# A two-block transformer kernel whose stage ends are reordered by token half, with five weight buffers instead of three

## The reference

```
x = layer_norm(ALPHA*x + rwkv7_time_mix(x)) ; x = layer_norm(ALPHA*x + swiglu_ffn(x))      # block 0
x = layer_norm(ALPHA*x + moba_attention(x)) ; x = layer_norm(ALPHA*x + swiglu_ffn(x))      # block 1
n = rmsnorm(x); z = n @ w_in -> conv branch, top-k attention branch, gates
h = x + (g_conv*y_conv + g_attn*y_attn) @ w_mix_out
h = h + cross_attention(rmsnorm(h), rmsnorm(mem)) @ wx_o
h = h + square(relu(rmsnorm(h) @ w_ff1)) @ w_ff2
return rmsnorm(h)
```

## Time and profile before

| | |
|---|---|
| median of 3 runs | 1526.9 us (1525.79 to 1529.86) |
| the profiled execution, its own time | 1531.04 us |
| its span, first to last instruction | 1528.9 us |
| mean granted TensorE clock | 0.965 |
| busy: PE, DVE, ACT, POOL | 1414.8, 882.3, 635.4, 78.6 us |
| weights and other data moved | 204.96 MB |

### The profile page before, as it was taken

The page is one execution under the profiler, slowest core; times in us unless marked ns, Lnnn a source line. Parts: engine busy times, 40 slices in busy tenths (PEclk is TensorE's granted clock), DMA queues, the critical chain, the costliest instruction groups (busy, mean ns, idle before and its releaser), DMA issues.

```text
span 1528.9 us, 21626 instructions
## 1 busy us (share of the span) xinstructions
PE 1414.8 (93%) x9280; PEld 1266.8 (83%) x9280; DVE 882.3 (58%) x1277; ACT 635.4 (42%) x899; POOL 78.6 (5%) x44
## 2 busy tenths in 40 slices
PE   7998999997899998999899999799988888799997
PEld 4676998996799997876689999798978887599996
DVE  4268426335644446555464444698998755465554
ACT  1342342433434433444453343534344545554443
POOL 0011120001200002100020000100000000000000
PEclk9999999998899999999999999898999999999999
DMA  9422000003555553623065555554543434255651
GB/s 287 139 73 83 1 29 1 1 29 110 166 193 193 180 192 107 211 83 111 28 227 192 188 193 166 161 157 131 166 145 111 156 120 129 91 184 175 195 192 69
DMA packets 154383, 204.96 MB, mean 134 GB/s; under 512 B 7440, under 2 KB 128400, under 8 KB 154160
## 3 DMA queue, kind: packets, MB, share of 16 engines
q1 hardware_dynamic: 154288, 203.59, 40.7%
HBM read 202.53 MB, written 1.05 MB: 133 GB/s over the span
## 4 chain that ended last, share of the span: by engine, by line
PE 69%; DVE 21%; ACT 6%; DMA 2%; issue 2%; DVEq 0%; SPq 0%; ACTq 0%
PE PS L468 16%; PE PS L469 16%; PE PS L470 16%; DVE PH L1963 6%; DVE WL L1541 4%; PE PS L756 3%; PE PS L743 3%; PE PS L760 2%; PE PS L659 2%; ACT WH L1082 2%; DMA RG<-in_ffn_w_in 1%; PE PS L604 1%; PE PS L709 1%; DVE PA L1775 1%; DMA RG<-in_moba_w_qkv 1%
## 5 line engine op out<-in xcount | busy, mean ns | idle before, releaser
L1541 DVE TENSOR_TENSOR WL<-RG,WH 128x2048 fp32r<-128x2048 f32 x163 | 372.5, 2290 | 246.1 <-ACT WH L1082 246.1
L468 PE MATMUL PS<-AH,WH 128*128 128x256 f32 x1664 | 482.7, 290 | 13.6 <-DVE AL L1568 9.5
L469 PE MATMUL PS<-AL,WH 128*128 128x256 f32 x1664 | 477.8, 287 | 0.0
L470 PE MATMUL PS<-AH,WL 128*128 128x256 f32 x1664 | 477.2, 287 | 0.0
L1082 ACT ACTIVATE WH<-RG 128x2048 fp32r<-128x2048 f32 x164 | 311.9, 1907 | 134.1 <-PE PS L470 87.9
L468 PEld LDWEIGHTS PS<-AH,WH 128*128 128x128 f32 x1664 | 326.1, 196 | 21.0 <-issue 11.8
L469 PEld LDWEIGHTS PS<-AL,WH 128*128 128x128 f32 x1664 | 326.3, 196 | 1.6 <-issue 0.2
L470 PEld LDWEIGHTS PS<-AH,WL 128*128 128x128 f32 x1664 | 326.0, 196 | 0.0
L468 PE MATMUL PS<-WH,HH 128*128 128x512 f32 x304 | 118.8, 391 | 0.0
L469 PE MATMUL PS<-WL,HH 128*128 128x512 f32 x304 | 118.8, 391 | 0.0
L470 PE MATMUL PS<-WH,HL 128*128 128x512 f32 x304 | 118.4, 389 | 0.0
(11 more groups left out here) (272 smaller groups left out, 1796.1 us busy)
## 6 DMA issues: line engine op xcount, KB each, us to landing
RG<-in_ffn_w_in SPq DMA_DIRECT2D x44, 1024.0 KB, 5.1
RG<-in_w_ff SPq DMA_DIRECT2D x32, 1024.0 KB, 5.4
RG<-in_w_in SPq DMA_DIRECT2D x30, 1024.0 KB, 5.2
RG<-in_ffn_w_down SPq DMA_DIRECT2D x22, 1024.0 KB, 4.9
RG<-in_moba_w_qkv SPq DMA_DIRECT2D x12, 1024.0 KB, 5.9
RG<-in_w_rkv SPq DMA_DIRECT2D x7, 1024.0 KB, 5.5
PA<-in_w_rkv SPq DMA_DIRECT2D x5, 1024.0 KB, 5.2
RG<-in_w_o SPq DMA_DIRECT2D x4, 1024.0 KB, 6.2
```

The lines of the kernel that those rows point to most:

```text
L468: e.matmul(o, lh, rh, start=start, stop=False)
L469: e.matmul(o, lh, rl, start=False, stop=False)
L470: return e.matmul(o, ll, rh, start=False, stop=stop)
L1541: v.tensor_tensor(WL[:, lo_n % NW, :], ring(SPLIT[lo_n]), WH[:, lo_n % NW, :].bitcast(F32), ALU.subtract).then_inc(s_lo, 1)
```

## The change

Six things change together.

1. Every stage end finishes the first half of the tokens before the second. `wo2`/`wo3`, `mo2`/`mo3`, `mx2`/`mx3`, `xo0`/`xo1`, and the last two down pieces of each FFN run as (piece a, half 0), (piece b, half 0), (piece a, half 1), (piece b, half 1).
2. DVE norms half 0 at once, then takes the remainder of the next stage's first weight, then norms half 1. The RMS norms work on one half at a time; DVE scales both halves (before, ACT scaled the second).
3. The memory unit that stood before the transposes of `ln0`, `ln1`, `ln2` now stands between the two halves. Its PSUM bank is another, and a wait on its copy-out inside the transposes is gone.
4. All pieces use five ring buffers, in a tensor of their own.
5. The final norm is per half, with one DVE instruction for scale and gain; POOL takes no part.
6. The DMA scratch of the program is set to 256 (it pays for the two buffers).

```diff
-    _k = _i % 5 if _n in EARLY else _i % 3
+    _k = _i % 5
...
-        RG = ctx.enter_context(nc.sbuf_tensor("RG", [128, 3, 2048], F32))
+        RG = ctx.enter_context(nc.sbuf_tensor("RG", [128, 5, 2048], F32))
...
-        MEM_AT = [PS[3][:, 0:256], PS[4][:, 0:256]] * 3 + [PS[3][:, 0:256], PS[2][:, 0:256]]
+        MEM_AT = [PS[5][:, 0:256], PS[4][:, 0:256]] * 4
...
+            def token_last(names, banks, nk=8):
+
                 for tt in range(2):
+                    for kp, name in enumerate(names):
+                        if tt == 0:
+                            split_ready(name)
+                        token_piece(name, banks[tt], tt, kp, nk)
+
+            def to_chan(name, src, banks, between=None):
+                for tt in range(2):
+                    if tt and between is not None:
+                        mem_unit(between)
...
-                        if tt == 0 and k == (4 if name == 'nmix' else 6) and name in MEM_BEFORE:
-                            e.wait_ge(s_mkvo, MEM_BEFORE[name])
...
+                    if 1 <= j < n - 1:
+                        down(f, n, j - 1, 0, mem_units)
+                        down(f, n, j - 1, 1, mem_units)
+                for tt in range(2):
+                    down(f, n, n - 2, tt, mem_units)
+                    down(f, n, n - 1, tt, mem_units)
...
-            token(('wo2', 'wo3'), (5, 7))
-            mem_unit(0)
-            to_chan('ln0', S1, [0, 1, 2, 3])
+            token_last(('wo2', 'wo3'), (5, 7))
+            to_chan('ln0', S1, [0, 1, 2, 3], 0)
...
-            def rms_scaled(q):
-                s.wait_ge(s_rv, q + 1)
-                s.activation(ST[:, 60:62], ST[:, 60:62], ACT.Sqrt, bias=0.0, scale=1.0).then_inc(s_rsd, 1)
-                s.wait_ge(s_rr_, q + 1)
-                s.activation(S1[:, 1, :], H[:, 1, :], ACT.Copy, bias=0.0, scale=ST[:, 61:62]).then_inc(s_na, 1)
+            def rms_std(q, tt):
+                s.wait_ge(s_rv, 2 * q + tt)
+                s.activation(ST[:, 60 + tt:61 + tt], ST[:, 60 + tt:61 + tt], ACT.Sqrt, bias=0.0, scale=1.0).then_inc(s_rsd, 1)
...
                 v.wait_ge(s_ho, half_mm)
                 ln_part(0, 0)
-                piece_done(first)
-                ln_part(1, 0)
                 v.wait_ge(s_ho, half_mm + 1)
                 ln_part(0, 1)
                 ln_scale(q, 0)
+                ahead(f'ln{q}', 1)
+                piece_done(first)
+                ln_part(1, 0)
                 piece_done(second)
                 ln_part(1, 1)
                 ln_scale(q, 1)
...
+            def final(tt):
...
+                for h in range(2):
+                    sl = slice(h * 512, h * 512 + 512)
+                    v.scalar_tensor_tensor(out=S1[:, tt, sl], in0=H[:, tt, sl], scalar=ST[:, c], in1=ring('nfin')[:, sl],
+                                           op0=ALU.mult, op1=ALU.mult).then_inc(s_fin, 1)
...
-    nc = _bacc.Bacc("TRN2", target_bir_lowering=False, num_devices=1)
+    nc = _bacc.Bacc("TRN2", target_bir_lowering=False, num_devices=1, dynamic_dma_scratch_size=256)
```

More of the change, by code:

```diff
@@ L924, in tensor_program, with moba_out @@
             e.wait_ge(s_rp, 8)
-            for n in range(4):
+            def moba_out(n, tt):
                 kp, h = n // 2, n % 2
[L927 to L930, removed]
-                split_ready(f'mo{n}')
[L932 to L947, removed]
+                for k in range(4):
+                    kx = 4 * kp + k
+                    if tt == 0 and h == 0 and k % 2 == 0:
+                        e.wait_ge(s_tl, H_AT['mo'] + kx // 2 + 1)
+                    t = mm3(e, PS[4 + 2 * tt + h][:, :], act_kt(kx, tt), wsl(f'mo{n}', 512, k, 0, 512), kx == 0, kx == 7)
+                if tt:
+                    t.then_inc(s_wdone, 1)
+                elif kp:
+                    t.then_inc(s_ho, 1)
+            for n in range(2):
+                split_ready(f'mo{n}')
+                step()
+                moba_out(n, 0)
+                step()
+                moba_out(n, 1)
+            step()
+            step()
+            step()
+            for tt in range(2):
+                for n in range(2, 4):
+                    if tt == 0:
+                        split_ready(f'mo{n}')
+                    moba_out(n, tt)
+            to_chan('ln2', S1, [0, 1, 2, 3], 4)
             mem_unit(5)
             ffn(1, True, 'ln2', 6)
+            e.wait_ge(s_ly, 7)
             mem_unit(6)
@@ L1064, in tensor_program @@
             e.wait_ge(s_oa, 20)
-            token(('xo0',), (4, 6), 4, ready=H_AT['xo'])
-            token(('xo1',), (5, 7), 4)
+            for tt in range(2):
+                for n in range(2):
+                    if tt == 0:
+                        split_ready(f'xo{n}')
+                    token_piece(f'xo{n}', 4 + 2 * tt + n, tt, 0, 4, H_AT['xo'] if (tt, n) == (0, 0) else None)
             to_chan('nffn', S1, [0, 1, 2, 3])
@@ L1399, in scalar_program @@
             layer_norm(3)
-            for tt, h in ((1, 0), (1, 1), (0, 0), (0, 1)):
-                s.wait_ge(s_h3v if tt else s_h3g, h + 1)
-                square(tt, h)
-            rms_scaled(1)
+            for tt in range(2):
+                for h in range(2):
+                    s.wait_ge(s_h3v if tt else s_h3g, h + 1)
+                    square(tt, h)
+                    if (tt, h) == (1, 0):
+                        rms_std(1, 0)
+            rms_std(1, 1)
+            mem_out(6)
+            mem_out(7)
             chan_out('nmix', XT, [0, 1, 2, 3])
@@ L1495, in scalar_program @@
             ahead('mx1')
-            for n, (tt, h) in enumerate(((0, 0), (1, 0), (0, 1), (1, 1))):
-                if n == 2:
-                    ahead('mx2')
-                s.wait_ge(s_hx, n + 1)
-                square(tt, h)
-            rms_scaled(2)
+            ahead('mx2')
+            for tt in range(2):
+                for h in range(2):
+                    s.wait_ge(s_hx, 2 * tt + h + 1)
+                    square(tt, h)
+                rms_std(2, tt)
             chan_out('nx', XT, [0, 1, 2, 3])
@@ L1517, in scalar_program @@
             ahead('xo0')
-            for n, (tt, h) in enumerate(((0, 0), (1, 0), (0, 1), (1, 1))):
-                s.wait_ge(s_hx, n + 5)
-                square(tt, h)
-            rms_scaled(3)
+            for tt in range(2):
+                for h in range(2):
+                    s.wait_ge(s_hx, 2 * tt + h + 5)
+                    square(tt, h)
+                rms_std(3, tt)
             chan_out('nffn', XT, [0, 1, 2, 3])
@@ L1524, in scalar_program @@
             sqrt_table()
-            for n in range(4):
-                s.wait_ge(s_hx, n + 9)
-                square(n // 2, n % 2)
-            rms_scaled(4)
+            for tt in range(2):
+                for h in range(2):
+                    s.wait_ge(s_hx, 2 * tt + h + 9)
+                    square(tt, h)
+                rms_std(4, tt)
         def vector_program(v):
@@ L1691, in attention @@
                 t.then_inc(s_pn, 1)
+            def final(tt):
+                c = slice(60 + tt, 61 + tt)
+                v.wait_ge(s_sq, 18 + 2 * tt)
+                own_dve(v.tensor_tensor(ST[:, 6 + tt:7 + tt], ST[:, 2 * tt:2 * tt + 1], ST[:, 2 * tt + 1:2 * tt + 2], ALU.add))
+                own_dve.done()
+                v.tensor_scalar(ST[:, c], ST[:, 6 + tt:7 + tt], 1.0 / C, EPS, ALU.mult, ALU.add).then_inc(s_rv, 1)
+                v.wait_ge(*landed('nfin'))
+                v.wait_ge(s_rsd, 8 + tt)
+                own_dve(v.reciprocal(ST[:, c], ST[:, c]))
+                own_dve.done()
+                for h in range(2):
+                    sl = slice(h * 512, h * 512 + 512)
+                    v.scalar_tensor_tensor(out=S1[:, tt, sl], in0=H[:, tt, sl], scalar=ST[:, c], in1=ring('nfin')[:, sl],
+                                           op0=ALU.mult, op1=ALU.mult).then_inc(s_fin, 1)
             def add_h(tt, h):
@@ L2101, in vector_program @@
                 add_h(n // 2, n % 2)
[L2102 to L2110 removed]
+                if n % 2:
+                    final(n // 2)
         def gpsimd_program(g):
```

114 lines of the change are left out of this document (47 added, 67 removed).

## The result

The changed kernel took 1506.7 us (median of 4 runs, 1501.5 to 1508.2), the kernel before 1527.0 (4 runs): a ratio of 0.986, 95% interval 0.983 to 0.989, which is 20.3 us less. The forecast was 1506. Beside later experiments on another chip it came to 1506.4 us (ratio 0.985, 0.983 to 0.987). The profiled execution took 1507.1 us with a span of 1505.2, against 1531.0 and 1528.9 before: 23.7 us less span, where the prediction's sum said 21.

What follows compares the result with a forecast made beforehand. PE, busy 93% of the span, was taken to bound the kernel, so only its 114 us idle could shrink. Waits of 18.3 us plus 2.7 of clock made 21 us, from 1526.9 to 1506 us; range 1497 to 1516.

Steps and rivals of the forecast that it cites:

- The waits of the norm: At the stage ends, PE's transposes waiting for normed tokens: savings of 3.6 us at wo, 4.1 at mo, 1.5 at mx.
- after FFN 1: Two norms in a row where PE waits 6.74 us: 4.6 us saved, bounds 2 and 6.7.
- At the end: End of the program: only half 1 left to finish, DVE done at 1523.7 instead of 1525.71, 2.0 us saved.
- What is late next: At wo, the activation remainder (1.78 us wait) follows the second transposes by a fixed time and moves with them, unchanged.
- Stage xo: Transposes save 1.1 us, a new 1.0 us wait for the second weight piece: 0.1 us net, bounds -1 and +1.1.
- up to 1 us: At mo, the second piece must be split 2.7 us sooner; PE at full rate might wait up to 1 us.
- The clock: Half-rate stretches of PE after stage ends: one of five goes, 2.7 us, from bounds of 0 to 14 us.
- a sign of error: In the changed profile, PE busy time falling by much more than 3 us would mean the clock did it.
- The ring: At wo, five buffers land the first FFN weights early, taking their cast off ACT, which half 0's readiness before T needs.
- only the first half gains: Rival: half 1's chain sets the stage end, behind weight remainders on DVE; gain 8 us, 1519 us, chance 0.12.
- The smaller DMA scratch: Rival: it slows the loads, PE waits 1.7 us for each of 44 pieces, 1580 us; chance 0.03.
- The clock staying up: Rival: half-rate stretches go with the waits, some 8 us more than counted, 1498 us; chance 0.13.

Runs made afterwards that it cites:

- x_pool_small: Changed kernel with POOL's sum H after the norms cut from instructions of 1024 columns into 256; 1490.5 us, ratio 0.976 to the kernel before.
- a_xo_old: Changed kernel with PE's old order at stage xo alone (xo0 for both halves, then xo1); 1503.6 us, ratio 0.984 to the kernel before.
- x_early_wl: Changed kernel with the casts and weight remainders of xo1 and mo3 moved ahead; 1504.6 us, ratio 0.984 to the kernel before.
- a_ring3: Changed kernel with three ring slots instead of five from wo on; 1510.7 us, ratio 0.988 to the kernel before.
- b_ring5: Kernel before with the five-slot ring alone and the room for it, old orders kept; ratio 0.992 to the kernel before.
- x_warm: Changed kernel with 120 dummy transposes of a constant filling PE's idle time at stage ends; 1497.1 us, ratio 0.980 to the kernel before.

## Why the prediction was right, and where it was not

**The waits of the norm.** Right in kind everywhere: half 0 does not wait at wo, after FFN 0, mo, mx and xo, half 1 not at the first three, and at wo every time worked out from rows came to within 0.3 us. The sizes are 0.5 to 1.2 us small, but for xo. The largest, after FFN 1, was 5.8 for 4.6: I let half 1's gain instructions start later than they did and worked the first transposes out 9.6 us behind T, and they stood 8.5 behind it. At the end DVE was through 2.4 us sooner, for 2.0 said, and the output after it took 2.4 us where I had put the same 3.2: the last store was no longer held behind another. The rest lies in PE's busy time, in which the sum had no term at the stage ends but the transposes of mx and xo: eight transposes that took 1.7 us at half rate take 1.1.

**What is late next.** I said the activation remainder comes a fixed time after the second transposes, unchanged. It does: at wo the matmul behind the last such wait starts 11.3 us after the second transposes (385.47 to 396.77), before 11.4 (389.45 to 400.81). But unchanged it is only in time, not as a wait: PE was granted half its clock from 389.7 to 393.1 before, ran the transposes and the memory unit at full rate now, and came sooner to remainders that were no sooner. Its waits for them at wo are 0.53, 1.80 and 1.82 us where they were 0.95 and 1.78. After FFN 0 I said that earlier loads would give only 0.2 us there because POOL stands beside DVE; the wait of 3.44 us for 3.77 confirms it, and `x_pool_small` confirms the reason. I treated this as a fixed cost of the kernel; it was a larger reserve than most terms of the sum.

**Stage xo: the step that failed.** The sum gave it 0.1 us, with a lower bound of -1; it cost 1.8. I had PE at half rate in its first 12 matmuls, as the trace before shows. In the changed kernel it ran them at full rate, 3.0 us (1295.23 to 1298.23) instead of 4.3, and came that much sooner to a remainder that was no sooner: a wait of 2.35 us for 1.0. The wait then put it on half rate, 1.7 us more. `a_xo_old` and `x_early_wl` both give the loss back. At mo the prediction had named the same risk ("up to 1 us") and set it to 0; it was 0.86.

**The clock.** This term was too small, and the total is right partly by luck. Forecast were 18.3 us of waits and 2.7 of clock; measured are 12.6 us less idle time and 11.1 less busy time. Between the stage ends, where nothing hides it, the clock gave 4.0 us. The other 7.1 lie at the stage ends, and there a part was taken back by the longer waits for remainders, 7.0 us more in all; how much, no run separates. Nor was it "one stretch gone": after wo the loss shrank from 2.9 us to 1.6, after FFN 0 from 2.8 to 1.7, three in the attention and at the start of mo went (at 639, 663 and 741 us) and one came (704), and one that costs 2.2 us appeared at the start of FFN 1. I had set as a sign of error a PE busy time that falls by much more than 3 us, "then the clock did it"; it fell by 11.1, so the sign was a good one and it showed. The transposes of normed tokens alone fell from 17.9 to 12.7 us of busy time.

The prediction says that the wait of 3.21 us at mo brought no half rate, since the next stage's matmuls ran at full rate. It had not looked at the instructions between them, the transposes and the memory unit. The trace before, as the earlier trace rows:

```profile
761.80:765.10 3.30, 3.25 (x12) 0.50 0.02 5
```

So that wait was followed by half rate too.

**The ring.** The prediction says that half 0 "needs" the cast off ACT and so the ring. At wo and after FFN 0 that is wrong: `a_ring3` has half 0 in time there. At mo it holds: without it the halves wait 1.8 and 0.9 us. And the ring alone brings 11 to 12 us, which the prediction did not see, because it took the old order of the norm as given: DVE stood behind a weight remainder until 381.15, and earlier loads free it.

**The rivals.** That only the first half gains is refuted by the second transposes without a wait. The smaller DMA scratch did not slow the loads: `b_ring5` has it and is faster by what its waits say. The clock staying up did not come with the change, but `x_warm` shows that it was to be had.

## What to carry to other kernels

Before a chain of small steps is reordered, look at what each of its instructions takes alone and what it takes in place; here one engine's long instructions held another's short ones, and cutting them to a quarter brought 14 to 16 us more where the whole change had brought 20. Split what a change gained into idle and busy time of the engine: a total that agrees can hide two terms that do not. Two remedies for one wait do not add up, so measure each alone before crediting either, and after each fix ask which buffer is now freed last. A wait that is shortened also moves the clock behind it, in both directions, so a new need for a buffer has to be timed at PE's full rate.

## What the hardware showed that I had not expected

A two-input instruction of DVE that starts while one of POOL runs ends 0.55 us behind that instruction of POOL: 512 columns take 0.69 us alone, 1.9 to 2.9 beside instructions of 1024 columns, 0.9 to 1.2 beside those of 256. One that starts ahead of POOL's is not held. The effect is mutual: POOL's 2.4 us for 1024 columns became 2.7 to 2.9 beside activation remainders and 4.3 to 4.5 beside weight remainders, and its 0.7 us for 256 columns became 2.8 beside the latter.

Waits of PE of 1.5 to 2.4 us with matmuls between them were followed by half rate at wo, mo and xo. With dummy transposes in those waits (`x_warm`) the granted clock stayed at 1.00 behind all three.
